# RWKV-7 core of a two-layer trunk: each level of the triangular inverse moves only the 32 columns it changes

## The reference, cut to what matters

```python
def step(s, inp):
    rt, wt, kt, vt, at, bt = inp
    sa = jnp.einsum('bhvk,bhk->bhv', s, at)
    s = s * wt[..., None, :] + sa[..., None] * bt[..., None, :] + vt[..., None] * kt[..., None, :]
    return s, jnp.einsum('bhvk,bhk->bhv', s, rt)
```

## Time and profile before

| | us |
|---|---|
| median of 3 runs | 3773.24 (3772.99 to 3790.44) |
| the profiled execution's own time | 3779.17 |
| its span, first to last instruction | 3777.6 |
| mean granted TensorE clock in it | 0.848 of full |

### The profile page before, as it was taken

How to read it: one execution, slowest core, us unless ns; L and a number is a source line. 1 busy time by engine, 2 the same in 40 slices (tenths; PEclk the granted TensorE clock), 3 DMA queues, 4 the chain that set the end, 5 groups by cost and what they waited for, 6 DMA issues and landing times. The chain is left out here.

```text
span 3777.6 us, 55814 instructions
## 1 busy us (share of the span) xinstructions
PE 2790.7 (74%) x23142; PEld 1396.8 (37%) x23142; DVE 887.1 (23%) x1895; ACT 524.7 (14%) x1076; POOL 485.4 (13%) x697
## 2 busy tenths in 40 slices
PE   4499955467678877878849577777787677877776
PEld 0144433233342222222224376676775322222121
DVE  0105034551021111111040254554452100000000
ACT  0100022211110000000020133333331100000000
POOL 0000000430101111111010222222221011111111
PEclk9799987788878888888879789988898688878888
DMA  9512100001349888989412200000001689888895
GB/s 385 225 67 86 48 0 0 1 0 61 122 169 358 350 353 361 365 359 364 186 38 78 98 12 12 12 12 12 12 12 53 267 352 362 349 349 355 353 354 209
DMA packets 180032, 676.08 MB, mean 179 GB/s; under 512 B 28568, under 2 KB 46784, under 8 KB 175344
## 3 DMA queue, kind: packets, MB, share of 16 engines
q1 hardware_dynamic: 128016, 487.87, 32.9%
q0 software_dynamic: 50688, 184.57, 12.5%
q10 hardware_dynamic: 1120, 0.48, 0.0%
HBM read 666.35 MB, written 6.49 MB: 178 GB/s over the span
## 5 line engine op out<-in xcount | busy, mean ns | idle before, releaser
L1372 PE MATMUL bank<-moe_w,moe_hidT 128*64 128x512 f32 (+1 forms) x1408 | 500.6, 847 | 223.5 <-DMA moe_w<-in_exp_w 209.6
L1350 PE MATMUL bank<-moe_w,moe_xT 128*64 128x512 f32 (+3 forms) x3072 | 633.4, 573 | 2.2 <-DVE moe_xT L1425 2.2
L1350 PEld LDWEIGHTS bank<-moe_w,moe_xT 128*64 128x64 f32 (+1 forms) x3072 | 203.2, 128 | 449.9 <-issue 447.2
L1474 POOL DMA_DIRECT2D moe_w<-in_exp_w x352 | 185.9, 528 | 1414.2 <-PE bank L1372 1320.8
L1372 PEld LDWEIGHTS bank<-moe_w,moe_hidT 128*64 128x64 f32 (+1 forms) x1408 | 98.6, 156 | 583.2 <-DMA moe_w<-in_exp_w 339.8
L1448 DVE COPY moe_rows<-bank 32x512 f32 (+1 forms) x96 | 65.9, 686 | 760.8 <-PE bank L1372 759.9
L1400 ACT ACTIVATE moe_silu<-bank 64x512 f32<-64x512 f32 (+3 forms) x96 | 46.2, 545 | 1332.2 <-PE bank L1350 1332.2
L392 PE MATMUL bank<-w_slab,mixT 128*128 128x512 f32 x384 | 166.2, 593 | 1.9 <-PE bank L392 1.6
L2057 PE MATMUL bank<-x_inv_and_t,p_prod 64*64 64x64 f32 x2560 | 156.8, 219 | 6.5 <-issue 5.7
L389 PE MATMUL bank<-mixT,w_slab 128*128 128x512 f32 x320 | 141.0, 602 | 12.0 <-DMA w_slab<-in_ab_w_in 10.9
L1819 DVE TENSOR_TENSOR x_inv_and_t<-bank,x_inv_and_t 128x512 f32<-128x512 f32 (+1 forms) x160 | 102.1, 638 | 195.3 <-PE bank L2057 194.6
(11 more groups left out here) (450 smaller groups left out, 3258.5 us busy)
## 6 DMA issues: line engine op xcount, KB each, us to landing
moe_w<-in_exp_w SPq DMA_DIRECT2D x512, 704.0 KB, 7.9
moe_w<-in_exp_w POOLq DMA_DIRECT2D x352, 512.0 KB, 8.8
ada_slab<-in_ada_w SPq DMA_DIRECT2D x32, 1536.0 KB, 12.8
w_slab<-in_ab_w_in SPq DMA_DIRECT2D x11, 2048.0 KB, 7.5
wo_slab<-in_ab_w_out SPq DMA_DIRECT2D x16, 512.0 KB, 3.7
rw_slab<-in_rw_wk SPq DMA_DIRECT2D x4, 1024.0 KB, 6.7
rw_slab<-in_rw_wv SPq DMA_DIRECT2D x4, 1024.0 KB, 5.0
rw_slab<-in_rw_wr SPq DMA_DIRECT2D x4, 1024.0 KB, 5.8
```

What stands on the lines that cost most here:

```text
L1350: mm = pe.matmul(g.ps[k][64 * m:64 * m + M, 0:hi - lo], xg[:, j, c, :], wa[:, c % RA, m, lo:hi], start=(c == 0), stop=(c == DC - 1))
L1372: mm = pe.matmul(g.ps[5 + m][64 * m:64 * m + M, :], hidt[:, c, :], wb[:, c % RB, 512 * m:512 * m + 512], start=(c == 0), stop=(c == FC - 1))
L1474: pool.dma_start(wb[:, c % RB, :], pick(w2)[c * P:(c + 1) * P, :]).then_inc(s_wb[c % RB], 16)
```

## The change

At a level only half of the columns of X change: in each pair of blocks the columns of block d (for X) and of block 1 - d (for its transpose). The change moves only those 32 columns through the array, instead of 64. Weights stay 64 x 64, and the number of MATMULs, their order and the banks stay as they were.

- `pmm` moves 32 columns of X, picked in runs of m, and packs the result in 32 columns.
- `pcopy` reads 128 elements per partition instead of 256 and writes them to their columns in a tile with one 64-column buffer per level, `p_prod` now [128, 5, 8, 64] per direction. The other columns have to be zero for the product that uses P whole as weights; they are cleared once, by two DVE memsets in the block ahead of the passes, beside POOL's memsets.
- `xmm` moves 32 columns of P and 32 of X^T.
- The add becomes two adds of 128 x 128 (one at the last level), each with its own count of the semaphore, so the waits count `added(n)` = n + min(n, 16). `pmm(n)` waits only for the first of the two adds of unit n - 4.
- X and its transpose swap places in `inv` for d = 1.

```diff
-        ah, rh, pp = two("a_hat", [P, T]), two("r_hat", [P, SEG]), two("p_prod", [P, NCH, LC])
+        ah, rh, pz = two("a_hat", [P, T]), two("r_hat", [P, SEG]), two("p_prod", [P, 5, NCH, LC])
...
+            @block.vector
+            def _(dve):
+                for z in pz:
+                    dve.memset(z[:, :, :, :], 0.0)
...
+            X, XT = (0, 1), (1, 0)
+            part = lambda x, lv, h: x.rearrange("p (b h r) -> p b h r", h=2, r=2 << lv)[:, :, h, :]
+            runs = lambda x, lv: x.rearrange("p (b r) -> p b r", r=2 << lv)
+            added = lambda n: n + min(n, 16)
...
-                        half = g.ps[XB(n)][:, :].rearrange("p (c k t) -> p c k t", k=2, t=LC)
-                        k = slice(0, 2) if lv < 4 else slice(1, 2)
-                        dve.tensor_tensor(inv[d][:, c:c + LAT, k, :], half[:, :, k, :], inv[d][:, c:c + LAT, k, :], ALU.add).then_inc(S["xadd"], 1)
+                        half = g.ps[XB(n)][:, 0:SEG].rearrange("p (c k t) -> p c k t", k=2, t=LC // 2)
+                        for k, h in ((X[d], d), (XT[d], 1 - d)) if lv < 4 else ((XT[d], 1 - d),):
+                            x = inv[d][:, c:c + LAT, k, :].rearrange("p c (b h r) -> p c b h r", h=2, r=2 << lv)[:, :, :, h, :]
+                            dve.tensor_tensor(x, half[:, :, k, :].rearrange("p c (b r) -> p c b r", r=2 << lv), x, ALU.add).then_inc(S["xadd"], 1)
...
-                            act.activation(pp[d][:, c:c + LAT, :], C3(g.ps[n % 2][:, 0:LAT * LC]), ACT.Copy).then_inc(S["pcopy"], 1)
+                            m = 2 << lv
+                            act.activation(pz[d][:, lv, c:c + LAT, :].rearrange("p c (b h r) -> p c b h r", h=2, r=m)[:, :, :, d, :],
+                                           g.ps[n % 2][:, 0:LAT * LC // 2].rearrange("p (c b r) -> p c b r", c=LAT, r=m), ACT.Copy).then_inc(S["pcopy"], 1)
...
-                                mm = pe.matmul(g.ps[n % 2][r, c * LC:(c + 1) * LC], nlev[d][r, lv % 2, c0 + c, :], inv[d][r, c0 + c, 0, :], start=True, stop=True)
+                                mm = pe.matmul(runs(g.ps[n % 2][r, c * HC:(c + 1) * HC], lv), nlev[d][r, lv % 2, c0 + c, :], part(inv[d][r, c0 + c, X[d], :], lv, d), start=True, stop=True)
...
-                                    pe.matmul(g.ps[XB(n)][r, o:o + LC], inv[d][r, c0 + c, 1, :], pp[d][r, c0 + c, :], start=True, stop=True)
+                                    pe.matmul(runs(g.ps[XB(n)][r, o(X[d])], lv), inv[d][r, c0 + c, XT[d], :], part(pz[d][r, lv, c0 + c, :], lv, d), start=True, stop=True)
...
-                                mm = pe.matmul(g.ps[XB(n)][r, o + LC:o + 2 * LC], pp[d][r, c0 + c, :], inv[d][r, c0 + c, 1, :], start=True, stop=True)
+                                mm = pe.matmul(runs(g.ps[XB(n)][r, o(XT[d])], lv), pz[d][r, lv, c0 + c, :], part(inv[d][r, c0 + c, XT[d], :], lv, 1 - d), start=True, stop=True)
```

More of the change, by code:

```diff
@@ L1802, in core @@
                         W(dve, "mm1", i, 8, 4 * d + 2)
-                        dv.do(dve.tensor_tensor(inv[d][:, :, 0, :], C3(g.ps[B + 1][:, :]), many(g.lev[:, 1 - d, 0, :], NCH), ALU.mult))
-                        dv.do(dve.tensor_tensor(inv[d][:, :, 1, :], nt[d][:, :, :], many(g.lev[:, d, 0, :], NCH), ALU.mult))
+                        dv.do(dve.tensor_tensor(inv[d][:, :, X[d], :], C3(g.ps[B + 1][:, :]), many(g.lev[:, 1 - d, 0, :], NCH), ALU.mult))
+                        dv.do(dve.tensor_tensor(inv[d][:, :, XT[d], :], nt[d][:, :, :], many(g.lev[:, d, 0, :], NCH), ALU.mult))
                         dv.join(dve)
@@ L1978, in apart @@
                     pe.sem_inc(S["apart"], 1)
+                HC = LC // 2
                 def heads(bank, col0, lhs, rhs_, chunks):
@@ L2030, in pmm @@
                         if n >= 4:
-                            W(pe, "xadd", i, NU, n - 3)
+                            W(pe, "xadd", i, added(NU), added(n - 4) + 1)
                         elif n % 2 == 0:
@@ L2048, in xmm @@
                         if n >= 2:
-                            W(pe, "xadd", i, NU, n - 1)
+                            W(pe, "xadd", i, added(NU), added(n - 1))
                         apart()
                         for c in range(LAT):
-                            o = 2 * c * LC
+                            o = lambda k: slice((2 * c + k) * HC, (2 * c + k + 1) * HC)
                             if lv < 4:
                                 for r in HALF:
-                                    pe.matmul(g.ps[XB(n)][r, o:o + LC], inv[d][r, c0 + c, 1, :], pp[d][r, c0 + c, :], start=True, stop=True)
+                                    pe.matmul(runs(g.ps[XB(n)][r, o(X[d])], lv), inv[d][r, c0 + c, XT[d], :], part(pz[d][r, lv, c0 + c, :], lv, d), start=True, stop=True)
                             for r in HALF:
-                                mm = pe.matmul(g.ps[XB(n)][r, o + LC:o + 2 * LC], pp[d][r, c0 + c, :], inv[d][r, c0 + c, 1, :], start=True, stop=True)
+                                mm = pe.matmul(runs(g.ps[XB(n)][r, o(XT[d])], lv), pz[d][r, lv, c0 + c, :], part(inv[d][r, c0 + c, XT[d], :], lv, 1 - d), start=True, stop=True)
                         mm.then_inc(S["xmm"], 1)
@@ L2096, in core @@
                         B = 4 * d
-                        W(pe, "xadd", i, NU, NU - 2 * (1 - d))
+                        W(pe, "xadd", i, added(NU), added(NU - 2 * (1 - d)))
                         W(pe, "nkv", i, 2, d + 1)
@@ L2101, in core @@
                             for r in HALF:
-                                mm = pe.matmul(g.ps[B + c // LAT][r, c % LAT * P:(c % LAT + 1) * P], inv[d][r, c, 1, :], rhs[d][r, c, :, :].rearrange("p k t -> p (k t)"), start=True, stop=True)
+                                mm = pe.matmul(g.ps[B + c // LAT][r, c % LAT * P:(c % LAT + 1) * P], inv[d][r, c, XT[d], :], rhs[d][r, c, :, :].rearrange("p k t -> p (k t)"), start=True, stop=True)
                         mm.then_inc(S["aumm"], 1)
```

## The result

The changed kernel takes 3812.9 us (median of 4 runs, 3809.5 to 3822.0), the kernel before 3777.3 beside it on the same chip: the ratio is 1.0092, 95% interval 1.0060 to 1.0125, some 35 us slower. The forecast was 73 us slower, 3846, with a range of 3766 to 3890. Direction and range hold; the size is twice too large. The profiled execution took 3822.0 us (span 3820.4, mean clock 0.835 where before had 0.848), so it is the slowest of its four runs, and its 42.8 us over the profiled span of before are 7 more than the medians give.

The account below looks back on a forecast made before the run. PE was taken to bound the inverse by its 29.4 ns step per MATMUL. Terms 0 (step) + 70 (clock) + 0 (copies, adds) + 3 (memsets) = 73 us on the median 3773 gave 3846, range 3766 to 3890.

Parts of the forecast that it names:

- The bound: Inside the inverse of each pass: PE sets the time, through the 29.4 ns step of each of 7168 MATMULs.
- Part 1: The inverse's MATMULs with 32 moving columns: weights stay 64 wide, so 0 saved at equal clock; bounds 0 and 91 us.
- rival B: Inverse's MATMULs: the step follows the moving columns, up to 91 us saved, 3685 to 3750 us; chance 0.13.
- Part 2: Inverse in all 8 passes: clock falls to 1.2 GHz behind a gap, 70 us slower; bounds 24 and 150, without fall 0.
- the `tok` pair: Two groups of 64-column matmuls for the scaled keys, where the fallen clock was to return, after 329 MATMULs per pass.
- no change: Whole kernel: a difference under 0.5% (19 us); chance 0.35.
- Part 3: ACT's copies, DVE's adds and the finer semaphore count in the inverse: both engines wait for PE, so 0.
- Part 4: Two DVE memsets in the block ahead of the passes: net 3.0 us slower, once; bounds 0 and 4.1.
- A: Inverse: the step stays and the clock holds, so no effect but the memsets, 3776 us; chance 0.35.
- C: Level 0 of the inverse: strided picks in runs of two lengthen the steps, 42 us slower, 3818; chance 0.04.

Follow-up runs that it names:

- e7: Kernel before, with 32 weight and 32 moving columns in the inverse's MATMULs, half of each product and all updates left out; ratio 1.0007.
- e2: Kernel before, with the first 32 contiguous columns moved, copied and added instead of 64; ratio 1.0032.
- e4: Kernel before, with 16 contiguous columns moved, copied and added instead of 64; ratio 1.0473.
- e8: Kernel before, with 32 weight columns and all 64 moving in the inverse, half of each product left out, adds to a scratch tile; ratio 0.9992.
- e1: Changed kernel with PE moving all 64 columns again, copies and adds still of the 32 changed columns; ratio 1.0034 to the kernel before.
- e12: Changed kernel with 64 moving columns again and one semaphore count per unit for DVE's adds; ratio 1.0019 to the kernel before.
- e5: Changed kernel with one semaphore count per unit, behind both of DVE's adds; ratio 1.0048 to the kernel before.
- e10: Changed kernel without PE's early wait for the second direction's identity add behind its first 16 MATMULs; ratio 1.0070 to the kernel before.
- e11: Changed kernel with one count per unit and without PE's early wait for the second direction's identity add; ratio 1.0006 to the kernel before.
- e3: Kernel before, with 48 contiguous columns moved, copied and added instead of 64; ratio 1.0001.

## Why the prediction was right, and where its size was wrong

*The bound.* Right that PE sets the inverse, and that everything between the passes stands behind it. Incomplete: the 29.4 ns step isn't all of it. The portions of instructions, which the prediction saw as two gaps of 0.75 and 0.92 us, are a second floor right beside the first (e7).

*Part 1, no saving at equal clock.* Right. Forecast 29 ns, measured 29.1. e2 to e4 show the step held by the weight side, and e8 that the moving side holds it as well when it is the wide one. The upper bound of 91 us (rival B) would not have come even with a smaller step: e7 has 16.6 ns, the very number of that reading (16.7), and a ratio of 1.0007, with 23.0 us at 1.2 GHz among what it lost.

*Part 2, the clock falls.* The mechanism was right in kind: whole stretches at 0.50, behind a gap, and without them (e1, e12) no time is lost in the passes. The term was mis-sized, 70 us against 34.0 in the passes. Four parts of it:
- Length. I took one fall per pass that stays until the `tok` pair, 329 MATMULs at the low level, 17 to 19 us per pass. Measured: 85.3 / 8 = 10.7 us. Most stretches at half last 3.4 to 7 us; only two reach 17 us, behind the identity add of the first pass and the sixth. And the last pass has none.
- End. I let the clock come back with the 64-column matmuls of the `tok` pair. It doesn't go by them: five stretches (48 us) are over before the pair, one of 10.2 us goes on through all of it, and six (27 us) begin only behind it. The pair in the third pass, 64 MATMULs of 64 columns at 1.2 GHz:

```profile
2405.31 3.72 PE L2001 MATMUL bank<-eye,k_bar 64*64 64x64 f32 x64
```

- Price. I took 29.4 ns per MATMUL where my own row gave 53.5 - 29.0 = 24.5. Measured: 52.9 - 29.1 = 23.8. With it the 85.3 us cost 85.3 x 23.8 / 52.9 = 38 us; the inverses grew by 34.6. With 24.5 the forecast for part 2 would have been 57 us.
- Place. I named the gap at the fourth to fifth unit. The falls begin behind DVE's identity add (five passes) and behind late instructions, mostly near MATMUL 590 of the inverse, where the gap grew from 0.25 us to 0.88 in most passes (start to start). Both gaps in the fourth pass, PEld of the changed kernel; here the clock held behind the first and fell 0.8 us behind the second:

```profile
2477.66 0.57 PEld L2056 LDWEIGHTS bank<-x_inv_and_t,n_levels 64*64 64x64 f32 x16 [1.87 <-issue]
...
2504.04 0.19 PEld L2072 LDWEIGHTS bank<-x_inv_and_t,p_prod 64*64 64x64 f32 x2 [0.71 <-issue]
```

That the change is slower by more than the prediction's 0.5% is in part luck. e5, with the same 32 columns and one count, is 0.48% slower, just inside what the prediction called no change. The finer count, which the prediction put at 0, carried the result over that line.

*Part 3, adds, copies and the count: 0.* Right for the adds and copies: both engines wait more than before. Wrong for the count, in a way the prediction didn't look for. It asked only whether a wait ends later, not what a wait costs PE in register instructions. With the clock at 1.00 the finer count costs nothing that the profiles show over the passes (e1 against e12); with it falling, 0.64%, 20 to 24 us (e10 against e11). Much of its cost is thus a part of the clock's: 53.8 us at 1.2 GHz against 17.1.

*Part 4, the memsets: +3.0.* Measured +3.8. The duration of 2.19 us is exact; the 0.48 us between them was missing, which makes 2 x 2.19 + 0.48 - 1.35 = 3.5.

*The rivals.* A (the clock holds) is out: only the last pass behaves so. B (the step follows the columns) is out, by the weight side, and behind it by the arrival of instructions. C (strided picks slow) is out: 29.1 ns with and without.

## What to carry to other kernels

Narrowing the moving side of a small matmul whose weight side is as wide buys no time and streams less per microsecond, which can cost the clock: so look first at the granted clock of the window and at each gap in it. Where waits that end in "issue" stand a fixed number of instructions apart, look whether PE's instructions come late by the instruction rows of the DMA queues; if they do, faster matmuls gain nothing, as in e7. Whether fewer of them would, no run shows. Look for waits on two producers where the next work needs one: deleting such a line was the only edit here that made the kernel faster.

## What the runs showed of the hardware that was not expected

- PE's instructions arrive 124 MATMULs with their loads at a time, 3.9 to 4.5 us apart, with steps of 29.6 ns and of 16.6 ns alike (before, e7). Each portion is one DMA packet of 16384 bytes, which takes about 1 us, and a PE that waited for it goes on 1.2 to 1.6 us behind its landing. The Trainium skill ("Runtime: NRT & Kernel Launch", section "Instruction fetch mechanics") has fetches in blocks of 256 instructions, "mostly hidden". The block agrees (124 + 124, and waits); hidden it isn't, with gaps of 0.2 to 1.3 us in the kernel before and of up to 2.3 us in e7.
- The granted clock stays at half through 37.5 us of matmuls without a pause (16 moving, 64 loaded; e4) and holds at 1.00 through gaps of 1.8 us when 64 move (before). The inverses spend 3.4 us at half with 48 moving columns, 29.8 with 32 and 421.7 with 16 (e3, e2, e4). With 32 moving and 32 loaded they spend 23.0 (e7), with 64 moving and 32 loaded none (e8).
- A step of 16.6 ns for fp32 matmuls with 32 weight and 32 moving columns in alternating corners (e7).
- A finer semaphore count, 76 register instructions of PE per pass instead of 42, costs 0.64% where the clock falls (e10 against e11) and nothing that the profiles show over the passes at a steady clock (e1 against e12).
